# Opening stage of a two-layer trunk: the scale vector as columns on TensorE, and x turned, normalized and split tile by tile

## The reference

```
cond = silu(c)                                      # (1, 2048)
mod = cond @ ada_w[i] + ada_b[i]                    # ada_w[i]: (2048, 6 * 2048)
sh1, sc1, g1, sh2, sc2, g2 = split(mod, 6)
h = rmsnorm(x, norm_mix[i]) * (1 + sc1) + sh1       # rmsnorm: x / sqrt(mean(x*x) + eps) * gain
y = mixer(h, ...)                                   # layer 0: h @ w_in first, w_in (2048, 3672)
x = x + g1 * y
```

## Time and profile before

| | |
|---|---|
| median of 3 runs | 2775.75 us (2767.36 to 2777.0) |
| profiled execution | 2772.71 us, of which the span is 2770.8 us |
| PE busy, weight loads busy | 93%, 75% of the span |
| DVE, ACT busy | 62%, 37% |
| first product of chunk 0 | 154.96 us after the start of the span |
| granted TensorE clock, mean | 0.955 of full |

### The profile page before, as it was taken

One profiled execution on the slowest core, in us unless ns is written; L12 is line 12 of the kernel. 1 busy time (PEld: TensorE's weight loads), 2 busy tenths in 40 slices (PEclk: granted clock), 3 DMA queues, 4 the chain that ended last, 5 costly groups with the idle time before them and its releaser, 6 DMA issues.

```text
span 2770.8 us, 29298 instructions
## 1 busy us (share of the span) xinstructions
PE 2581.2 (93%) x11766; PEld 2066.2 (75%) x11766; DVE 1720.6 (62%) x1398; ACT 1020.1 (37%) x947; POOL 3.2 (0%) x11
## 2 busy tenths in 40 slices
PE   5789877889999999999997999999999999999998
PEld 1368656567787788878876888878778788888886
DVE  6566637485766766676656666677677654445445
ACT  1033213244433333333344444444443333333333
POOL 0000000000000000000000000000000000000000
PEclk8789978699999999999998999999999999999999
DMA  8758645476687778777876888789678755655553
GB/s 316 284 203 283 199 151 211 152 257 214 234 312 281 265 251 304 268 268 250 296 215 142 230 183 214 188 237 316 225 252 297 262 187 182 196 182 196 183 185 118
DMA packets 255001, 636.54 MB, mean 230 GB/s; under 512 B 16858, under 2 KB 28084, under 8 KB 229428
## 3 DMA queue, kind: packets, MB, share of 16 engines
q1 hardware_dynamic: 254180, 629.89, 69.2%
q0 software_dynamic: 720, 5.24, 0.5%
HBM read 633.00 MB, written 2.10 MB: 229 GB/s over the span
## 4 chain that ended last, share of the span: by engine, by line
PE 83%; DVE 9%; DMA 3%; ACT 2%; issue 2%; SPq 1%; DVEq 0%; ACTq 0%
PE PS L909 24%; PE PS L911 24%; PE PS L910 24%; DVE WLO L1427 3%; DMA RAW<-in_ada_w 2%; DVE ACC L1440 1%; ACT WHI L554 1%; PE PS L1100 1%; PE PS L958 1%; PE PS L973 1%; PE PS L1130 1%; PE PS L954 1%; PE PS L1287 1%; PE PS L1331 1%; DMA RAW<-in_mla_w_ukv 1%
## 5 line engine op out<-in xcount | busy, mean ns | idle before, releaser
L909 PE MATMUL PS<-WHI,AHI 128*128 128x512 f32 x2120 | 835.2, 394 | 27.6 <-DVE WLO L1427 11.3
L911 PE MATMUL PS<-WHI,ALO 128*128 128x512 f32 x2120 | 828.2, 391 | 0.0
L910 PE MATMUL PS<-WLO,AHI 128*128 128x512 f32 x2120 | 827.7, 390 | 0.0
L1427 DVE TENSOR_TENSOR WLO<-RAW,WHI 128x2048 fp32r<-128x2048 f32 (+2 forms) x222 | 503.6, 2270 | 392.7 <-ACT WHI L554 392.3
L554 ACT ACTIVATE WHI<-RAW 128x2048 fp32r<-128x2048 f32 (+2 forms) x222 | 421.2, 1898 | 709.4 <-PE PS L911 650.2
L1921 DVE TENSOR_TENSOR WLO<-RAW,WHI 128x2048 fp32r<-128x2048 f32 x176 | 403.4, 2292 | 361.7 <-ACT WHI L788 361.1
L788 ACT ACTIVATE WHI<-RAW 128x2048 fp32r<-128x2048 f32 x176 | 337.4, 1917 | 590.9 <-PE PS L911 571.0
L909 PEld LDWEIGHTS PS<-WHI,AHI 128*128 128x128 f32 x2120 | 400.0, 189 | 114.4 <-issue 26.7
L911 PEld LDWEIGHTS PS<-WHI,ALO 128*128 128x128 f32 x2120 | 399.5, 188 | 84.2
L910 PEld LDWEIGHTS PS<-WLO,AHI 128*128 128x128 f32 x2120 | 399.6, 188 | 81.0 <-issue 0.2
L909 PE MATMUL PS<-WHI,GHI 128*128 128x512 f32 x960 | 382.1, 398 | 16.2 <-DVE GLO L1525 8.4
(11 more groups left out here) (289 smaller groups left out, 1519.3 us busy)
## 6 DMA issues: line engine op xcount, KB each, us to landing
RAW<-in_ffn_w SPq DMA_DIRECT2D x264, 1024.0 KB, 5.2
RAW<-in_ada_w SPq DMA_DIRECT2D x192, 1024.0 KB, 5.6
RAW<-in_fox_w_in SPq DMA_DIRECT2D x64, 1024.0 KB, 8.6
RAW<-in_even_w_in SPq DMA_DIRECT2D x28, 1024.0 KB, 5.3
RAW<-in_even_w_out SPq DMA_DIRECT2D x16, 1024.0 KB, 6.0
RAW<-in_fox_w_out SPq DMA_DIRECT2D x16, 1024.0 KB, 6.3
GROW<-in_ada_b POOLq DMA_DIRECT2D x4, 1024.0 KB, 5.5
RAW<-in_nsa_cmp_w_k SPq DMA_DIRECT2D x4, 1024.0 KB, 6.3
```

Source lines behind the costliest of these rows:

```text
L909: mm(dst(tb), xh, whi[:, k, :], start=first and k == 0, stop=False)
L910: mm(dst(tb), xh, wlo[:, k, :], start=False, stop=False)
L911: ins = mm(dst(tb), xl, whi[:, k, :], start=False, stop=last and k == nk - 1)
L1427: TT(m.w_view(m.WLO, u), m.w_view(m.RAW, u), m.w_view(m.WHI, u).bitcast(F32), ALU.subtract).then_inc(m["lo_ready"].sem, 1)
```

## The change

- The order of tiles in the opening stage stays a, r alternating, but two weight tiles of chunk 0 (w0, w1) are put in ahead of the last two pairs.
- The r tile becomes the stationary operand, 128 x 128 at a time, and one column of cond the moving one: 16 matmuls for each tile, and the scale arrives in PSUM as columns (L1132). The copy and the turning of the row are gone.
- x is turned as loaded (`x_raw`), two groups behind r4 and two behind r6. The inverse root comes ahead of the first a tile; it is spread over the partitions by one matmul with a diagonal, copied (RSP), and DVE multiplies the turned groups with it (XG).
- The bias pieces follow r7 to r12, with one PSUM bank in place of two.
- Scale and shift, high half and low half are done for each 128 features, and chunk 0 waits for each of these (`opening_unit`).
- The small loads and the positions are issued by ACT; x is loaded by SP right behind the first four tiles.
- The two a tiles of chunk 7 of even_in move to chunks 3 and 4.

```diff
-        self.prologue = [plan.unit("ar"[k % 2]) for k in range(2 * KT)]
-        self.even_in = [plan.chunk("even_in", i, rows(win, 512 * i + (24 if i > 4 else 0), 512), 2) for i in range(7)]
+        for kt in range(KT):
+            if kt >= KT - 2:
+                src, nk, cols, kt0 = rows(win, 0, 512)[kt - (KT - 2)]
+                self.opening.append(plan.unit("w", src=src, nk=nk, cols=cols, kt0=kt0))
+                self.prologue.append(self.opening[-1])
+            self.prologue += [plan.unit("a"), plan.unit("r", vec=(0, SC1), kt=kt)]
+        self.even_in = [plan.chunk("even_in", i, rows(win, 512 * i + (24 if i > 4 else 0), 512), (2, 2, 2, 3, 3, 2, 2)[i],
+                                   early=self.opening if i == 0 else ()) for i in range(7)]
...
         def bias_piece(q):
             wait("oh_ready", q)
-            if q >= 2:
-                wait("bias_kept", q - 2)
+            if q:
+                wait("bias_kept", q - 1)
...
+        def x_raw(g):
+            if g == 0:
+                wait("x_full", "all")
+            if g >= 2:
+                wait("xg_ready", g - 2)
+            for j in range(4):
+                for tb in range(2):
+                    at = 512 * g + P * j
+                    ins = turn(m.x_turned(g)[:, j, P * tb:P * tb + P], m.X[:, tb, at:at + P], m.ID)
+            m["t_done"].tick(ins, ("norm", 0, g))
...
-        for k, u in enumerate(m.prologue[1::2]):
+        side = {4: lambda: (x_raw(0), x_raw(1), spread_both()), 6: lambda: (x_raw(2), x_raw(3))}
+        side.update({7 + q: lambda q=q: bias_piece(q) for q in range(6)})
+        for k, u in enumerate([u for u in m.prologue if u.kind == "r"]):
             pe.wait_ge(m.raw_full[u.s % RING], 16 * (u.s // RING + 1))
-            for q in range(4):
-                ins = mm(m.PS[0:1, q, :], m.COND[:, k:k + 1], m.RAW[:, u.s % RING, 512 * q:512 * q + 512], start=k == 0, stop=k == KT - 1)
-            m["row_used"].tick(ins, k)
-            if k % 2 and 3 <= k <= 13:
-                bias_piece((k - 3) // 2)
+            for j in range(KT):
+                ins = mm(m.PS[:, 6, j:j + 1], m.RAW[:, u.s % RING, P * j:P * j + P], m.COND[:, u.kt:u.kt + 1],
+                         start=k == j == 0, stop=k == KT - 1 and j == KT - 1)
+            m["row_used"].tick(ins, ("ada", k))
+            if k in side:
+                side[k]()
         finish((0, SH1))
-        wait("modulated", 0)
-        norm(0)
...
+        inverse_root(("norm", 0), 2, D)
+        for tb in range(2):
+            ins = TS(m.DG[:, tb, :], m.ID, m.RS[:, 3, tb:tb + 1], None, ALU.mult)
+        m["diag_ready"].tick(ins, 0)
+        shifts = [u for u in m.prologue if u.kind == "a"]
+        for u in shifts[:3]:
+            ada(u)
+        steps(0)
+        ada(shifts[3])
+        wait("spread_done", 0)
+        link(V.tensor_copy(m.RSP, m.PS[:, 5, 0:T]))
+        for g in range(4):
+            wait("t_done", ("norm", 0, g))
+            m["xg_ready"].tick(TT(m.XG[:, 4 * g:4 * g + 4, :], m.x_turned(g), m.RSP.unsqueeze(1).to_broadcast([P, 4, T]), ALU.mult), g)
+            if g == 1:
+                ada(shifts[4])
+        ada(shifts[5])
+        steps(1)
+        for q in range(6):
+            ada(shifts[6 + q])
+            keep_bias(q)
+            if q < 4:
+                steps(q + 2)
...
+        for u, v in zip(m.opening, shifts[14:]):
+            lo(u)
+            ada(v)
+        wait("row_used", ("ada", KT - 1))
         finish((0, SH1))
...
+        for kt in range(KT):
+            if kt + 1 < KT:
+                modulated(kt + 1)
+            wait("tf_ready", ("norm", 0, kt))
+            split_lo(("norm", 0, kt), m.ALO[:, kt, :], m.TF[:, kt % 4, :], m.AHI[:, kt, :])
```

More of the change, by code:

```diff
@@ L343, in make_plan @@
         self.norm_of = {"out0": 1, "down02": 2, "out1": 3, "down12": "final"}
-        order = [("norm", 0, g) for g in range(4)] + [("even_in", i) for i in range(7)] + [("cmp", 0), ("cmp", 1)]
+        order = [("even_in", i) for i in range(7)] + [("cmp", 0), ("cmp", 1)]
         order += [("mla", i) for i in range(6)] + [("rope", i) for i in range(3)] + [("mla", 6), ("mla", 7)] + [("even_o", g) for g in range(4)]
@@ L458, in _ @@
         m["con_full"].tick(sp.dma_start(m.CON[:], t["const_table"][:, :]), 0, 16)
[L459 to L468, removed]
         for u in m.prologue[:RING]:
             load(u)
[L471 to L478, removed]
         for tb in range(2):
             m["x_full"].tick(sp.dma_start(m.X[:, tb, :], t["x"][0, P * tb:P * tb + P, :]), "all", 16)
-        m["x_full"].tick(sp.dma_start(m.GB[:], t["nsa_gate_b"][0:1, :].to_broadcast([P, 24])), "all", 16)
-        m["x_full"].tick(sp.dma_start(m.FB[0:16, 0:1], t["fox_f_b"].rearrange("a h -> h a"), allow_slow_non_contiguous=True), "all", 16)
         for u in m.prologue[RING:]:
             load(u)
-        load_chunks(m.even_in)
+        for c in m.even_in:
+            for u in c.units:
+                if u not in m.opening:
+                    load(u)
         for u in m.cmp_in[0]:
@@ L657, in enter @@
             keep_x(n, 3)
[L659 to L677, removed]
+        for at, src in ((V_C, t["c"].rearrange("a (k p) -> (a k) p", p=P)),
+                        (V_MIX, t["norm_mix"].rearrange("a (k p) -> (a k) p", p=P)),
+                        (V_FFN, t["norm_ffn"].rearrange("a (k p) -> (a k) p", p=P)),
+                        (V_QN, t["mla_q_norm"].rearrange("a (k p) -> (a k) p", p=P)),
+                        (V_KVN, t["mla_kv_norm"].rearrange("a (k p) -> (a k) p", p=P)),
+                        (V_FQ, t["fox_q_norm"]), (V_FK, t["fox_k_norm"]), (V_PK, t["nsa_cmp_pos_k"][0])):
+            m["vec_full"].tick(act.dma_start(m.VROWS[0][at:at + src.shape[0], :], src), "all", 16)
@@ new lines, in _ @@
+        for g in range(4):
+            m["pos_full"].tick(act.dma_start(m.RB[32 * g:32 * g + 32, :], t["rel_bias"][:, :]), "all", 16)
+        wait("zeroed", "shifted")
+        for g in range(4):
+            m["pos_full"].tick(act.dma_start(m.RBS[32 * g + 1:32 * g + 32, :], t["rel_bias"][0:31, :]), "all", 16)
+        m["bias_full"].tick(act.dma_start(m.GB[:], t["nsa_gate_b"][0:1, :].to_broadcast([P, 24])), "all", 16)
+        m["bias_full"].tick(act.dma_start(m.FB[0:16, 0:1], t["fox_f_b"].rearrange("a h -> h a"), allow_slow_non_contiguous=True), "all", 16)
@@ L681, in _ @@
+        wait("x_full", "all")
+        for i in range(4):
+            x_squares(("norm", 0), i)
+        root(("norm", 0), 2)
         wait("ang_ready", 0)
@@ L683, in _ @@
         m["trig_ready"].tick(A(m.COS[:], m.ANG[:, 2:4, :], ACT.Sin), 0)
-        wait("x_full", "all")
-        for i in range(4):
-            x_squares(("norm", 0), i)
-        norm(0)
+        for u in m.opening:
+            hi(u)
+        wait("gs_ready", 0)
+        for kt in range(KT):
+            m["hi_split"].tick(A(m.AHI[:, kt, :], m.XG[:, kt, :], ACT.Identity, scale=m.GS[:, 0, kt:kt + 1], bias=m.SHM[:, 0, kt:kt + 1]), ("norm", 0, kt))
         def even_first(c):
@@ L1093, in bias_piece, with spread_both @@
             m["bias_sum"].tick(ins, q)
+        def x_raw(g):
+            if g == 0:
+                wait("x_full", "all")
+            if g >= 2:
[5 more added lines that the diff above has]
+            m["t_done"].tick(ins, ("norm", 0, g))
+        def spread_both():
+            wait("diag_ready", 0)
+            m["spread_done"].tick(mm(m.PS[:, 5, 0:T], m.ONE, m.DGF, start=True, stop=True), 0)
@@ L1648, in _ @@
         wait("gk_turned", 0)
+        wait("bias_full", "all")
         gk = m.PS[:, 4, 0:T].rearrange("p (b n) -> p b n", b=2)
```

100 lines of the change are left out of this document (51 added, 49 removed).

## The result

The changed kernel takes 2809.88 us (median of 4 runs, 2802.04 to 2820.34), the kernel before 2776.38 (4 runs, 2767.36 to 2778.66): a ratio of 1.0129, 95% interval 1.0089 to 1.0169. It is slower by 33.5 us. The forecast was 2819, 43 us slower. The profiled execution has a span of 2806.9 us against 2770.8, +36.1.

The account below looks back on a forecast made before the run. Bound until 113 us by loads and scale tiles, then to 155.0 by a chain without loads. Profiled 2772.7 + 45.4 (first product) + 4 (gap) - 6 (moved tiles) = 2816, plus 3.0 for the median: 2819 us; range 2783 to 2836.

Parts of the forecast that it names:

- main case: Opening stage: scale tiles at half clock and waits between engines delay the first product by 45.4 us; 2819 us, chance 0.67.
- the two bounds worked out for it: Whole kernel: main case with cheaper or dearer pieces, loads, gap and other terms, -11 or +17; 2808 to 2836 us.
- T0: Start of the first product after the opening stage; forecast 200.4 us against 155.0, +45.4.
- A tile of 7.0 us: Opening stage: each r tile as 16 one-column matmuls runs at half clock, 7.0 us, against 3.61 before at full clock.
- the sign that I had named: Opening stage: L1132 at 7 us a tile with the clock at 0.50 from 20 to 200 us.
- the clock rises inside each tile: Rival, opening stage: column matmuls raise the clock, a tile takes 5.2 us, 20 less in all; 2799 us, chance 0.13.
- The order costs more than the form: Opening stage: later a and r tiles wait for slots; from free slot to r tile start takes 7.4 us.
- The round from r7 on: Opening stage: r tile, piece, BIAS copy, comparisons, a tile, load; 23.9 us for two tiles, where two took 11.4.
- the bias piece at half clock: TensorE, behind r7 to r12: taken as 2.0 us, between 1.4 and 2.7.
- The start: VectorE's first a tile: root and small diagonal ahead of it move its start from 27.5 to 29.0 us, 28.5 to 31 possible.
- The gap ahead of unit 2: TensorE behind the first product: units 0 and 1 end before VectorE's work, a gap of about 4 us, 0 to 6.
- The moved a tiles: Chunk 7's two a tiles in chunks 3 and 4: the gate's finish comes earlier, giving back 4.8 to 7 us, taken as 6.

Follow-up runs that it names:

- the kernel with wide matmuls: The changed kernel with an unused 512-column bf16 matmul added ahead of every second column matmul of the scale; 2835.11 us in one run.
- that one pair: Two scale tiles at 108.82 us, taking 10.62 us, in the changed kernel with its side work spread over the tiles; median 2774.16 us, ratio 1.0004.
- the kernel with columns alone: The kernel before with only the scale tile changed to one-column matmuls, order, norm and loads kept; median 2789.35 us, ratio 1.0061.
- the table above: First product's start in four kernels: columns 201.61 us in the changed kernel's order, 162.48 with side work spread; rows 190.26 and 143.72.
- both parts undone: The changed kernel with the scale as a row again and its side work spread over the tiles; median 2758.12 us, ratio 0.9936.

## Why the prediction was right

The main case held, in its mechanism and nearly in its size. The median lies only 1.9 us above the lower of the two bounds worked out for it (2808 and 2836): behind T0 the errors of size all went one way, and up to T0 they mostly cancelled.

- **A tile of 7.0 us.** Measured 6.9 to 7.0 in every kernel with columns, but for r5 of the kernel after (4.09), r5 of the kernel with wide matmuls and that one pair. Every tile on the chain of the kernel after took 6.9 to 7.0. The stretches of the kernel after show 0.55 and 0.50 from 80 us on; the sign that I had named, 0.50 from 20 us on, did not come, since the column reads 1.00 up to 66 us while three tiles take 20.64 us. In the kernel with columns alone it reads so for the whole stage:

```profile
110.00:147.00 37.00, 37.00 (x259) 37.00 (x258) 13.55 (x8) 0.00 (x0) 0.66 (x1) 1.00 0.80 288
170.00:177.00 7.00, 3.00 (x7) 2.45 (x8) 6.50 (x4) 3.33 (x2) 0.00 (x0) 1.00 0.28 77
```

  But in the second of these stretches, with the same 1.00, its chain has

```profile
175.62 0.43 PE PS L909
...
177.65 0.23 PE PS L909
```

  0.43 us is half clock and 0.23 full. This trace has no change of the clock on record until later, so there I read the clock from durations. "TensorE: Matmul & The Clock Gate" of the Trainium skill, which lets continuous work bring the full clock (Why this matters for your kernels), is contradicted by this form: 110 us without a pause at 6.9 us a tile. The rival "the clock rises inside each tile" came true for r5 alone, off the chain.
- **The order costs more than the form.** Held, and shown both ways by the table above: 39.1 of 46.7 with columns. The round from r7 on was 23.0 us where 23.9 was forecast. The term that was most off is the bias piece at half clock, 1.3 to 1.4 us, not 2.0. r9, r11, r13 began at 121.60, 144.39, 163.20, forecast 121.8, 145.7, 165.4; r14 and r15 at 177.36 and 185.60, forecast 176 and 184. So from r13 to r15 3.8 us were lost again: r14 began 11.9 us behind the end of a12, where 10.2 were priced for w0's load and the next, and a14 waited for w0's low half until 176.57. TensorE stood still 8.46, 10.71, 6.62 and 6.40 us ahead of r6, r7, r9 and r11 as forecast (5 to 11), but only 0.98 ahead of r13, and the DMA share was 0.33 and then 0.53, near the 0.5 forecast only in the second stretch.
- **The start.** This is the term that was mis-sized. a0 began at 31.92, forecast 29.0, above the bound of 31. I had priced the vectors' loads on ACT at 0 to 2 us. They now run beside the large loads, and the chain of the kernel after begins with them:

```profile
5.01 9.66 DMA TF<-in_ada_b
14.81 1.21 PE PS L1095 x4
...
21.06 1.49 DMA GROW<-in_rel_bias
```

  The last vector landed at 14.7 us, where the one matmul group waiting for it could start at 7.3 before, and the positions, issued behind the silu, were read at 22.57, against 20.16 before. That is 2.4 us; the root and the diagonal took 2.0 us (29.90 to 31.92) and not 1.5. Half of it came back, because two turned groups and the spread took 3.9 us and not 4.7, the clock rising among them, and three tiles and the load a little less too: r6 began at 77.37, forecast 76.0. "DMA: Bandwidth & Descriptors" of the Trainium skill (Queues, rings and completion order) has each DMA engine take packets from SP's and ACT's rows in turn; that agrees with small loads that are slowed by large ones on the other row, though no run here separates it from other causes.
- **The gap ahead of unit 2.** Forecast 4 us, 0 to 6; it was 0. A round of scaling and low half took VectorE 0.66 us, not 0.85, and from 202 us on TensorE was busy without a break. Instead the clock rose later behind T0 (at about 207.5, 6 us on, where before it took 3), and the second chunk began 1.6 us later behind T0 than before.
- **The moved a tiles.** Forecast 6; measured 5.5 alone, and 5.5 from T0 to the convolution in the kernel after, the 1.6 included. TensorE's timeline of the kernel after, against the earlier trace rows:

```profile
374.22 3.05 PE L954 MATMUL PS<-ACC,CON 128*128 128x512 f32 x4 [3.58 <-DVE GROW L1478]
...
380.34 30.22 PE L1157 MATMUL PS<-RAW,BF 128*30 128x256 f32 x128 [2.78 <-DVE BF L1700]
```

  The wait ahead of L954 was 8.88 for an a tile; it is 3.58 now. The convolution, at 339.15 before, is behind by 41.2 us.
- **What was not forecast.** From there to the end 5 us come back: +40.5 at 398 us of before, +36.5 at 748, +36.1 at 2656. In the middle stages the clock is not full throughout, and where it is low shifts with everything before. One sum shows it, the first row from the chain of before, the second from that of after:

```profile
520.31 6.99 PE PS L958 x32
```

```profile
560.68 5.14 PE PS L958 x32
```

  The stretches of 400 us behind the convolution say the same: the clock's mean is 0.85 before and 0.87 after.

```profile
345.00:745.00 400.00, 334.36 (x1533) 265.98 (x1532) 249.24 (x283) 135.64 (x225) 0.53 (x1) 0.85 0.59 204
```

```profile
386.00:786.00 400.00, 337.42 (x1562) 268.53 (x1561) 251.45 (x284) 136.90 (x226) 0.53 (x1) 0.87 0.59 205
```

  From T0 to the end, the 5.5 of the moved tiles left aside, the profiled executions of the other kernels range from 5.9 us less to 3.7 us more than the kernel before. So I count it as scatter, not as an effect of the change; that it is scatter was not shown by repeated traces of one kernel.

The sum of the errors: +1.3 at T0 (46.65 for 45.4), which is in part luck, since the error was +2.9 at a0, +0.7 at r7, -2.2 at r13 and +1.6 at r15; -3.5 for gap and moved tiles (-5.5 for +4 - 6); -5.1 in the middle stages; and -1.8 since the median stands 1.2 above the profiled execution (2808.73), not 3.0. That is -9.1: 2809.9 for 2819. One sum of the prediction is off: the terms named for the upper bound (eight loads and three pieces at 0.7 each, 2 for the gap, 2 for the positions, 3 for the chunks) add up to about +15, not +17; nothing hangs on it.

What stays open is why the clock stays low among the columns, with wide matmuls between them too, and why it rose behind turned groups in three of these kernels but not behind each. Nor was it tried what w0 and w1 ahead of the last pairs cost: TensorE stands still ahead of r14 for 7.17 us in the kernel after and 6.51 with both parts undone, against 1.52 before.

## What to carry to other kernels

Before work is put "beneath the loads", write down for each engine the order in which pieces are made and awaited. A ring of slots couples two engines, and a piece that VectorE awaits straight behind the TensorE tile that makes it turns hidden work into a round of load, tile, piece and sum. Put it one or two tiles ahead of its reader: here that alone was worth 39 us, and 46.5 with the scale as a row. And price a one-column matmul with a new weight at half clock unless the trace of that very place shows otherwise; a row of 512-column passes and a single turning at the end was cheaper.

## What the runs showed of the hardware

- One-column fp32 matmuls, each with a new 128 x 128 weight, stayed at 0.216 us a pass (6.9 us for 32) through 110 us of unbroken work, with only bias pieces between them, and through 26 us with wide bf16 matmuls among them. The same form takes 0.108 us at full clock. Behind two turned groups of x it ran at or near that in two kernels (r5: 4.09 us in the kernel after).
- Turning a row with K = 1 matmuls costs the same 6.98 us for 32 passes at half clock as 128 x 128 weights do (6.99), though each turning matmul moves one number against 128.
- In the trace of the kernel with columns alone the clock reads 1.00 throughout the opening stage, and in that of the kernel after up to 66 us, even where durations are those of half clock.
- The vectors' eleven small loads, issued by ACT beside six loads of 1 MB by SP, landed at 14.7 us; issued first by SP they let the matmuls that wait for them start at 8.33, and a0 at 11.74.
